# Recurrent chunks: the key and value tiles of four of eight heads turned by transposes

## The chip, the cores and the metric

One core of a Trainium2 chip runs the whole program in one launch. The metric is the device time of one execution in microseconds (us), the median of several runs. TensorE (PE) does matrix products and writes them to PSUM; its weight loads are shown apart as PEld. VectorE (DVE), ScalarE (ACT) and GpSimd (POOL) do the elementwise work; SyncE (SP) issues the DMAs. Each engine works through its own instructions in program order, and engines wait for one another by semaphores only.

## What is computed

Two layers of a first block (half an FFN, a mixer of pooling, convolution and neighbourhood attention, half an FFN) and then two layers of a second block (half an FFN, a mixer of three branches, attention over a memory, half an FFN), on 256 tokens of width 1024, in float32. The change touches one branch of the second block's mixer, the recurrence with 8 heads of 64 (`_rwkv_branch`):

```python
def step(state, inp):
    r_t, w_t, k_t, v_t, kk_t, a_t = inp
    sa = jnp.einsum('bhij,bhj->bhi', state, kk_t)
    state = (state * w_t[:, :, None, :]
             - sa[..., None] * (kk_t * a_t)[:, :, None, :]
             + v_t[..., None] * k_t[:, :, None, :])
    return state, jnp.einsum('bhij,bhj->bhi', state, r_t)
```

The kernel does not step through the 256 tokens. It takes them in 4 chunks of 64: within a chunk the products of keys with keys, the inverse of a triangular 64x64 matrix and the outputs are small matrix products, and a state of 64x64 per head goes from chunk to chunk.

## The kernel before, in words

Big products (FFN, projections) take each weight piece of 512 KB from DRAM into `raw`, ACT rounds it to a high part `w_hi` (L764), DVE or POOL computes the rest `w_lo` (L989), and PE forms three products per tile (L398 to L400, L414 to L416, L526 to L529).

The recurrence is `pe_rwkv` (L1742), `act_rwkv` and `dve_rwkv`; PE runs it once per layer of the second block, so twice, with 4 chunks each: 8 chunks. The 8 heads lie in pairs: head tile `t` (0 to 3) holds one head on partitions 0 to 63 and one on partitions 64 to 127. `HEADS` lists them as (t, first half), (t, second half), t by t, and every loop of a chunk goes in that order. An operand on the second half writes PSUM on partitions 64 to 127, so that all products of a chunk are 64 rows by 64 columns of the array, on one corner of it or on the opposite one.

A chunk goes through these stages on PE, in this order:

1. Turning (L1749 to L1753): for each head three 64x64 tiles (values `rz`, keys `rw_c[2]` and `rw_c[3]`) are multiplied with a 64x64 piece of the identity matrix in `const`, which leaves each tile's transpose in PSUM (banks 0 and 1). 24 products per chunk; the last raises `rw_turned`. ACT then copies them to `rw_tok` (L1852, L1854).
2. Grams (L1758 to L1763), products of keys with keys and queries, masked by DVE (L1911).
3. One piece of filling: `fill(1)` does a quarter of the gate projections that are to be done anyway, whole-array products at L398 to L400.
4. The chunk's right-hand side (L1780, L1781), which needs `rw_tok`, then five rounds of matrix powers and the inverse (L1789, L1791, L1799), each round with a quarter piece of filling between, while ACT and DVE copy the powers.
5. Outputs and new state (L1805 to L1827). After the last of them (`rw_y`, L1827) the turning of the next chunk follows in the program with one wait, for `rw_chunk_in`, which DVE raised long before.

Nothing in the order is planned at run time: the order on PE is the order of the program text.

Of the kernel before, what the change touches and what calls it, by code (L numbers as in the profile page):

```python
# [83 lines left out]
def const_layout():  # L84

    at, n = {}, 0
    for name, width in (("ident", P), ("na_mask", GRID), ("pool_cnt", 2 * S), ("causal", 2 * S), ("eps_ln", 1), ("eps_ln4", 1),
                        ("eps_rms", 1), ("eps_rms4", 1), ("eps_gn", 1), ("eps_0", 1), ("inv_freq", 1),
                        ("rope_sign", 1), ("halves", P), ("gla_full", 256), ("gla_half", P), ("strict", P),
                        ("lower", CHUNK), ("eye2", CHUNK), ("gather", 2), ("gather_g", 1),  # L90
                        ("spread", 512)):
        at[name] = n
        n += width
    return at, n


CONST, CONST_N = const_layout()
# [48 lines left out]
def build(nc, a, out, stop=None):  # L146
    ctx = ExitStack()
    with ctx:
        def sb(name, shape, dt=F32):
            return ctx.enter_context(nc.sbuf_tensor(name, shape, dt))  # L150
# [3 lines left out]
        def sem(name):  # L154

            if name not in sems:
                sems[name] = ctx.enter_context(nc.semaphore(name))
            return sems[name]
# [12 lines left out]
        ps = ctx.enter_context(nc.psum_tensor("ps", [P, 8, 512], F32))  # L171
# [5 lines left out]
        const = sb("const", [P, CONST_N])  # L177
# [44 lines left out]
        def cst(name, n, p=P):  # L222
            return const[0:p, CONST[name]:CONST[name] + n]

        ident = cst("ident", P)
# [1499 lines left out]
        W = CHUNK  # L1725
# [16 lines left out]
        def pe_rwkv(pe, fill):  # L1742
            pe.wait_ge(sem("rw_scaled"), 1)
            for n in range(CHUNKS):
# [4 lines left out]
                for t, o in HEADS:  # L1749
                    for b, src in enumerate((rz[o, 8 + t, 1 + n * W:1 + (n + 1) * W], rw_c[o, 2, t, :], rw_c[o, 3, t, :])):  # L1750
                        col = (b % 2) * 4 * W + t * W
                        mm = nc.tensor.matmul(ps[o, b // 2, col:col + W], src, const[o, CONST["ident"] + o.start:
                                              CONST["ident"] + o.stop], start=True, stop=True)  # L1753
                mm.then_inc(sem("rw_turned"), 1)
                if n:

# [1 line left out]
                for t, o in HEADS:  # L1758
                    for bank, keys in ((4, rw_bh), (6, rw_kh)):
                        nc.tensor.matmul(ps[o, bank, 2 * W * t:2 * W * (t + 1)].rearrange("p (a c) -> p a c", a=2),  # L1760
                                         keys[o, t, at], rw_pr[o, t, :, at], start=True, stop=True)
                    mm = nc.tensor.matmul(ps[o, 7, t * W:(t + 1) * W], rw_pr[o, t, 0, at], rw_bh[o, t, at], start=True,
                                          stop=True)  # L1763
# [4 lines left out]
                def power(i, t, o):  # L1768

                    return (rw_pow[o, 2 * (i % 2), t, :],  # L1770
                            rw_pow[o, 2 * (i % 2) + 1, t, :] if i else rw_g[o, 0, t, 0:W])
# [6 lines left out]
                for t, o in HEADS:  # L1778
                    x = ps[o, 7, t * W:(t + 1) * W]
                    nc.tensor.matmul(x, rw_c[o, 0, t, :], rw_st[o, t, :], start=True, stop=False)  # L1780
                    mm = nc.tensor.matmul(x, rw_g[o, 1, t, 0:W], rw_tok[o, 0, t, :], start=False, stop=True)  # L1781
                mm.then_inc(sem("rw_x"), 1)
                for i in range(1, POWERS + 1):
# [3 lines left out]
                    for t, o in HEADS:  # L1787
                        a, b = power(i - 1, t, o)
                        mm = nc.tensor.matmul(ps[o, 0, t * W:(t + 1) * W], b, a, start=True, stop=True)  # L1789
                        if i < POWERS:  # L1790
                            mm = nc.tensor.matmul(ps[o, 1, t * W:(t + 1) * W], a, b, start=True, stop=True)  # L1791
# [6 lines left out]
                    for t, o in HEADS:  # L1798
                        mm = nc.tensor.matmul(ps[o, 5, t * W:(t + 1) * W], power(i, t, o)[0], rw_t[o, (i - 1) % 2, t, :],  # L1799
                                              start=True, stop=True)  # L1800
# [13 lines left out]
                for t, o in HEADS:  # L1814
                    mm = nc.tensor.matmul(ps[o, 0, t * W:(t + 1) * W], rw_t[o, POWERS % 2, t, :], rw_x[o, t, :], start=True,
                                          stop=True)
# [3 lines left out]
                for t, o in HEADS:  # L1820
                    nc.tensor.matmul(ps[o, 5, t * W:(t + 1) * W], rw_tok[o, 1, t, :], rw_tok[o, 0, t, :], start=(t == 0),
                                     stop=False, skip_group_check=True)
                pe.wait_ge(sem("rw_u_taken"), n + 1)
                for t, o in HEADS:
                    y, state = ps[o, 4, t * W:(t + 1) * W], ps[o, 5, t * W:(t + 1) * W]
                    nc.tensor.matmul(y, rw_u[o, t, :], rw_g[o, 0, t, W:2 * W], start=False, stop=True, skip_group_check=True)
                    mm = nc.tensor.matmul(state, rw_tok[o, 2, t, :], rw_u[o, t, :], start=False, stop=True,  # L1827
                                          skip_group_check=True)
# [11 lines left out]
            for t in range(4):  # L1840
                o = ps[:, 6 + t // 2, (t % 2) * S:(t % 2 + 1) * S]
                nc.tensor.matmul(o, w_rgate[:, 0, t * P:(t + 1) * P], rz[:, 13, 1:], start=True, stop=False)
                mm = nc.tensor.matmul(o, w_rgate[32:64, 1, t * P:(t + 1) * P], rz[32:64, 14, 1:], start=False, stop=True)
# [141 lines left out]
        def _(pe):  # L1985
# [73 lines left out]
            for l in range(LAYERS):  # L2059
# [8 lines left out]
                pe_mla(pe, fill)  # L2068
                pe_gla(pe, fill)
                pe_rwkv(pe, fill)  # L2070

                pe.wait_ge(sem("att_out"), PAIRS)
# [748 lines left out]
```

## Time and profile before

| | us |
|---|---|
| median of 3 runs (lowest, highest) | 2659.61 (2659.55, 2663.37) |
| the profiled execution, by itself | 2660.73 |
| its span, first to last instruction | 2658.9 |
| what lies around the span in that execution | 1.8 |
| mean granted clock of TensorE | 0.997 |

A profile is one execution. A record of PE has a start, and an end that is modelled, so that the busy time of PE says that it had work in flight and not that the array was full; starts and the distances between them are the safer reading. A float32 product appears as two records (two passes over the array), with a weight load (PEld) each. "64\*64 64x64" is a record with 64 rows and 64 columns of weights, whose result is 64 partitions by 64 elements. The granted clock is 1.00 at 2.4 GHz and 0.50 at 1.2 GHz. "..." in a block of rows marks rows left out.

### The profile page before, as it was taken

How to read it: one execution, taken by the hardware profiler on the slowest of the kernel's cores; microseconds unless marked ns; L12 is line 12 of the kernel's file. 1: busy time of each engine (PE TensorE's matmuls, PEld its weight loads, DVE VectorE, ACT ScalarE, POOL GpSimd, SP SyncE). 2: the span in 40 equal slices, each digit the busy share in tenths (PEclk: the TensorE clock that was granted, in tenths of full speed). 3: DMA queues.
4: the chain of work that ended last, by engine and by line, in shares of the span. 5: the costliest groups of instructions: out<-in, count | busy, mean ns of one | idle time of the engine just before them, and what ended most of it. 6: DMA issues, size and time to landing. Idle time of an engine off the chain costs nothing.

```text
span 2658.9 us, 47077 instructions
## 1 busy us (share of the span) xinstructions
PE 2612.7 (98%) x18468; PEld 2302.3 (87%) x18468; DVE 1810.2 (68%) x2923; ACT 1386.2 (52%) x2186; POOL 218.4 (8%) x95
## 2 busy tenths in 40 slices
PE   9999999999999999999999999999999999999999
PEld 7889788888978888889999898888888999988887
DVE  6667766766777677767732856777775953475777
ACT  5456644544564454456524556446446642455544
POOL 0000000000000000015225000000003422300000
PEclk9999999999999999999999999999999999999999
DMA  8875466577546656663413655665674421564564
GB/s 254 235 195 170 134 189 190 177 225 200 173 134 190 190 151 205 190 190 113 123 49 119 198 168 156 191 190 176 189 213 128 133 84 51 176 201 138 176 189 134
DMA packets 613672, 444.52 MB, mean 167 GB/s; under 512 B 28224, under 2 KB 573536, under 8 KB 613024
## 3 DMA queue, kind: packets, MB, share of 16 engines
q1 hardware_dynamic: 613536, 442.62, 56.5%
q8 instruction: 96, 1.57, 0.2%
q14 instruction: 40, 0.33, 0.0%
HBM read 441.51 MB, written 1.05 MB: 166 GB/s over the span
## 4 chain that ended last, share of the span: by engine, by line
PE 88%; DVE 8%; ACT 1%; issue 1%; DMA 0%; POOL 0%; DVEq 0%; SPq 0%; ACTq 0%
PE ps L526 23%; PE ps L529 11%; PE ps L398 8%; PE ps L414 7%; PE ps L399 7%; PE ps L400 7%; PE ps L415 7%; PE ps L416 7%; DVE w_lo L989 2%; PE ps L1799 1%; PE ps L1789 1%; PE ps L711 1%; PE ps L1760 1%; PE ps L1791 1%; PE ps L749 1%
## 5 line engine op out<-in xcount | busy, mean ns | idle before, releaser
L989 DVE TENSOR_TENSOR w_lo<-raw,w_hi 128x1024 fp32r<-128x1024 f32 x700 | 855.9, 1224 | 396.8 <-ACT w_hi L764 395.4
L764 ACT ACTIVATE w_hi<-raw 128x1024 fp32r<-128x1024 f32 x796 | 840.1, 1056 | 455.2 <-PE ps L416 226.8
L526 PE MATMUL ps<-in_both,w_hi 128*128 128x512 f32 x2688 | 843.3, 395 | 1.3 <-DVE w_lo L989 1.3
L529 PEld LDWEIGHTS ps<-in_both,w_lo 128*128 128x128 f32 x2688 | 504.9, 188 | 117.7
L529 PE MATMUL ps<-in_both,w_lo 128*128 128x256 f32 x2688 | 528.1, 278 | 0.0
L398 PE MATMUL ps<-in_both,w_hi 128*128 128x256 f32 x1632 | 476.1, 292 | 20.2 <-DVE in_both L1060 7.4
L399 PE MATMUL ps<-in_both,w_hi 128*128 128x256 f32 x1632 | 462.8, 284 | 0.0
L400 PE MATMUL ps<-in_both,w_lo 128*128 128x256 f32 x1632 | 462.6, 283 | 0.0
L526 PEld LDWEIGHTS ps<-in_both,w_hi 128*128 128x128 f32 x2688 | 421.0, 189 | 14.8 <-DVE w_lo L989 2.5
L808 ACT ACTIVATE work<-ps 128x256 f32<-128x256 f32 x336 | 129.6, 386 | 524.5 <-PE ps L529 524.5
L989 POOL TENSOR_TENSOR w_lo<-raw,w_hi 128x1024 fp32r<-128x1024 f32 x90 | 217.9, 2429 | 2069.4 <-ACT w_hi L764 2069.4
L398 PEld LDWEIGHTS ps<-in_both,w_hi 128*128 128x128 f32 x1632 | 313.6, 192 | 30.3 <-issue 7.1
L399 PEld LDWEIGHTS ps<-in_both,w_hi 128*128 128x128 f32 x1632 | 313.7, 192 | 1.0 <-issue 0.5
L400 PEld LDWEIGHTS ps<-in_both,w_lo 128*128 128x128 f32 x1632 | 313.5, 192 | 0.0
L414 PE MATMUL ps<-w_hi,hid_hi 128*128 128x512 f32 x704 | 276.0, 392 | 2.2 <-DVE ps L1186 2.2
L415 PE MATMUL ps<-w_lo,hid_hi 128*128 128x512 f32 x704 | 274.6, 390 | 0.0
L416 PE MATMUL ps<-w_hi,hid_lo 128*128 128x512 f32 x704 | 274.0, 389 | 0.0
L1079 DVE TENSOR_TENSOR work<-ps,work 128x256 f32<-128x256 f32 x336 | 142.0, 423 | 96.4 <-ACT work L808 92.4
L416 PEld LDWEIGHTS ps<-w_hi,hid_lo 128*128 128x128 f32 x704 | 132.2, 188 | 28.6
L414 PEld LDWEIGHTS ps<-w_hi,hid_hi 128*128 128x128 f32 x704 | 132.0, 187 | 27.0 <-DVE ps L1186 3.5
L415 PEld LDWEIGHTS ps<-w_lo,hid_hi 128*128 128x128 f32 x704 | 132.2, 188 | 20.8
L1037 DVE TENSOR_TENSOR in_both<-arena,in_both 128x512 fp32r<-128x512 f32 x44 | 31.6, 744 | 89.3 <-ACT in_both L770 89.1
(362 smaller groups left out, 2837.7 us busy)
## 6 DMA issues: line engine op xcount, KB each, us to landing
raw<-in_w_ffn_in SPq DMA_DIRECT2D x176, 512.0 KB, 3.8
raw<-in_w_mix SPq DMA_DIRECT2D x108, 512.0 KB, 3.9
raw<-in_ffn_w_gate SPq DMA_DIRECT2D x88, 512.0 KB, 4.1
raw<-in_ffn_w_up SPq DMA_DIRECT2D x88, 512.0 KB, 3.8
raw<-in_ffn_w_down SPq DMA_DIRECT2D x88, 512.0 KB, 4.2
raw<-in_w_ffn_out SPq DMA_DIRECT2D x88, 512.0 KB, 4.2
raw<-in_w_in SPq DMA_DIRECT2D x40, 512.0 KB, 3.8
raw<-in_w_out SPq DMA_DIRECT2D x32, 512.0 KB, 3.6
```

The source lines that it names most:

```text
L398: nc.tensor.matmul(o, lh, rh, start=first, stop=False, **kw)
L399: nc.tensor.matmul(o, lh, rl, start=False, stop=False, **kw)
L400: return nc.tensor.matmul(o, ll, rh, start=False, stop=last, **kw)
L414: nc.tensor.matmul(o, left_hi[:, tok], right_hi, start=first, stop=False, **kw)
L415: nc.tensor.matmul(o, left_hi[:, tok], right_lo, start=False, stop=False, **kw)
L416: return nc.tensor.matmul(o, left_lo[:, tok], right_hi, start=False, stop=last, **kw)
L526: nc.tensor.matmul(bank.rearrange("p (a t) -> p a t", a=2), hi[:, k, :], in_both[:, k, :, :], start=(k == 0), stop=False, skip_group_check ...
L529: mm = nc.tensor.matmul(bank[:, 0:S], lo[:, k, :], in_hi[:, k, :], start=False, stop=(k == KD - 1), skip_group_check=True)
L764: nc.scalar.activation(w_hi[:, e % SPLIT, :], raw[:, e % RAW, :], ACT.Copy).then_inc(sem("split_high"), 1)
L808: nc.scalar.activation(part[:, j % 2, i, :], gate_up_bank(j, i)[:, S:2 * S], ACT.Copy)\
L989: eng.tensor_tensor(w_lo[:, e % SPLIT, :], raw[:, e % RAW, :], w_hi[:, e % SPLIT, :].bitcast(F32), ALU.subtract)\
L1079: nc.vector.tensor_tensor(o, gate_up_bank(j, i)[:, 0:S], part[:, j % 2, i, :], ALU.add).then_inc(sem("summed"), 1)
```

## The change

In the turning stage the heads on partitions 0 to 63 use TensorE's transpose instruction, with the same operands and the same place in PSUM; the heads on partitions 64 to 127 keep the product. The order of the 24 instructions stays, and so does the semaphore, which the last product (second half of t = 3) still raises.

```diff
                 for t, o in HEADS:
                     for b, src in enumerate((rz[o, 8 + t, 1 + n * W:1 + (n + 1) * W], rw_c[o, 2, t, :], rw_c[o, 3, t, :])):
                         col = (b % 2) * 4 * W + t * W
-                        mm = nc.tensor.matmul(ps[o, b // 2, col:col + W], src, const[o, CONST["ident"] + o.start:
-                                              CONST["ident"] + o.stop], start=True, stop=True)
+                        eye = const[o, CONST["ident"] + o.start:CONST["ident"] + o.stop]
+                        if o.start == 0:
+                            nc.tensor.transpose(ps[o, b // 2, col:col + W], src, eye)
+                        else:
+                            mm = nc.tensor.matmul(ps[o, b // 2, col:col + W], src, eye, start=True, stop=True)
                 mm.then_inc(sem("rw_turned"), 1)
```

Per chunk that makes 4 groups of 3 transposes and 4 groups of 3 products, in turn.

## Rows read from the trace of the kernel before

**Rows 1.** The page: busy time, share of the span, instructions; chain of work by engine.

```profile
span 2658.9 us, 47077 instructions
PE 2612.7 (98%) x18468; PEld 2302.3 (87%) x18468; DVE 1810.2 (68%) x2923; ACT 1386.2 (52%) x2186; POOL 218.4 (8%) x95
...
PE 88%; DVE 8%; ACT 1%; issue 1%; DMA 0%; POOL 0%; DVEq 0%; SPq 0%; ACTq 0%
```

**Rows 2.** Windows, four chunks of a layer: us, busy of PE, PEld, DVE, ACT, POOL, PEclk, DMA.

```profile
1316.50:1339.50 23.00, 23.00 (x500) 21.72 (x501) 8.77 (x19) 6.91 (x13) 8.01 (x4) 1.00 0.32 91
1339.50:1362.50 23.00, 23.00 (x510) 21.76 (x508) 8.39 (x20) 6.17 (x12) 4.73 (x2) 1.00 0.23 68
...
1385.50:1408.50 23.00, 23.00 (x510) 21.76 (x505) 8.19 (x17) 7.71 (x14) 7.47 (x3) 1.00 0.18 49
```

**Rows 3.** Waits in 1316.5 to 1408.5: who for whom, us in total, times, longest.

```profile
POOL w_lo L989 <- ACT w_hi L764: 67.5, 11, 13.0
ACT yT L1860 <- PE ps L1791: 22.0, 16, 2.1
...
ACT work L1852 <- PE ps L1752: 4.0, 4, 1.1
```

**Rows 4.** All records of line 1752 (turning), by operand: ns min/median/max, starts, form.

```profile
L1752 PE MATMUL ps<-const,arena x128: 218/218/268, 1316.5 to 2224.7; 64*64 64x64 f32 x128
L1752 PE MATMUL ps<-const,work x128: 218/218/218, 1316.7 to 2202.0; 64*64 64x64 f32 x128
L1752 PE MATMUL ps<-const,zT x128: 218/218/218, 1339.7 to 2225.0; 64*64 64x64 f32 x128
```

**Rows 5.** Timeline of PE at the second chunk's turning: start us, us, line, operands, records.

```profile
1339.45 0.33 PE L1827 MATMUL ps<-yT,work 64*64 64x64 f32 x4
1339.57 0.28 PE L1752 MATMUL ps<-const,arena 64*64 64x64 f32 x2
1339.68 0.22 PE L1752 MATMUL ps<-const,zT 64*64 64x64 f32 x1
1339.69 0.27 PE L1752 MATMUL ps<-const,arena 64*64 64x64 f32 x1
...
1339.92 0.22 PE L1752 MATMUL ps<-const,arena 64*64 64x64 f32 x1
...
1340.27 0.22 PE L1752 MATMUL ps<-const,arena 64*64 64x64 f32 x1
...
1340.97 0.27 PE L1760 MATMUL ps<-arena 64*64 64x128 f32 x1
1341.02 0.22 PE L1752 MATMUL ps<-const,zT 64*64 64x64 f32 x1
1341.08 0.27 PE L1760 MATMUL ps<-arena 64*64 64x128 f32 x1
1341.08 0.22 PE L1752 MATMUL ps<-const,zT 64*64 64x64 f32 x1
```

**Rows 6.** Timeline of PE, a turn by 16 transposes (L459), and what follows it.

```profile
1554.90 1.91 PE L459 MATMUL ps<-const,zT 128*128 128x128 f32 x16
1556.57 0.48 PE L398 MATMUL ps<-w_hi,in_both 128*128 128x512 f32 x1
```

**Rows 7.** Timeline of PE in four short stretches of line 1563 (products of two forms in turn).

```profile
2111.67 0.33 PE L1563 MATMUL ps<-arena 64*64 64x64 f32 x4
...
2111.93 0.33 PE L1563 MATMUL ps<-arena 64*128 64x64 f32 x2
...
2112.09 0.28 PE L1563 MATMUL ps<-arena 64*128 64x64 f32 x2
...
2112.30 0.27 PE L1563 MATMUL ps<-arena 64*64 64x64 f32 x2
```

**Rows 8.** Timeline of PE after the last chunk of the second layer, the first wait.

```profile
2256.91 0.28 PE L400 MATMUL ps<-in_both,w_lo 128*128 128x256 f32 x1
2258.58 0.39 PE L398 MATMUL ps<-in_both,w_hi 128*128 128x256 f32 x1 [1.39 <-POOL w_lo L989]
```

**Rows 9.** Windows as in rows 2: two turns by transposes, line 1563's stretch, what follows each.

```profile
978.95:983.77 4.82, 2.54 (x16) 1.65 (x16) 4.69 (x10) 2.94 (x7) 0.00 (x0) 0.94 0.01 3
983.77:986.68 2.91, 2.89 (x14) 2.89 (x14) 2.91 (x7) 2.91 (x6) 0.00 (x0) 0.51 0.56 175
986.68:989.59 2.91, 2.91 (x27) 2.91 (x26) 1.19 (x4) 2.17 (x6) 0.00 (x0) 1.00 0.36 97
200.44:204.53 4.09, 2.79 (x19) 1.93 (x18) 3.39 (x9) 3.76 (x9) 0.00 (x0) 1.00 0.14 40
204.53:207.40 2.87, 2.86 (x24) 2.87 (x25) 2.77 (x6) 2.87 (x6) 0.00 (x0) 1.00 0.43 130
2110.59:2114.01 3.42, 3.42 (x50) 2.88 (x49) 3.08 (x6) 3.36 (x7) 0.00 (x0) 1.00 0.02 5
2114.01:2117.40 3.39, 3.39 (x30) 3.39 (x29) 3.19 (x8) 1.25 (x3) 0.00 (x0) 1.00 0.94 273
...
2123.90:2130.10 6.20, 6.20 (x23) 5.42 (x24) 3.30 (x10) 6.16 (x8) 0.00 (x0) 0.50 0.59 168
```

## The prediction

> **What bounds the kernel now.** I read the page first: PE is busy 98% of the span, and 88% of the chain that ended last is PE [rows 1]. A mean over 2659 us says nothing about one stage, so the windows of the four recurrent chunks of a layer come next: each chunk is 23.0 us and PE has work in flight for all of them [rows 2]. The waits of that stretch name ACT, DVE and POOL as the ones that wait, mostly for PE; no line of that list has PE waiting [rows 3]. PE's order thus sets the length of a chunk, and each 0.1 us that PE's turning stage gets shorter or longer moves the end by as much. What ACT takes from the turning (L1852) waits for PE about 1 us per chunk, and PE needs its copies only after the grams and a piece of filling, so a later `rw_turned` makes no wait of its own: what comes after it on PE is delayed along with it.
>
> **How the turning runs now.** 384 records in 8 chunks are 48 per chunk for 24 products, two passes each [rows 4]. The timeline shows two streams side by side: after the start at 1339.57 the first half's tiles (each six passes of one head) begin anew at 1339.92 and 1340.27, so one half makes six passes in 0.35 us, 0.058 us per pass, and the other half makes its six in the same 0.35 us, a little behind [rows 5]. 48 passes therefore take only 24 passes' time: from 1339.57 to the last start at 1341.08, 1.51 us. There is no pause at either end: the state products before it (L1827) and the grams after it (L1760) overlap with it [rows 5], since all have the same 64\*64 form. In a layer's first chunk it is 0.05 us more, 1.56 us.
>
> **What the change removes.** 12 of the 24 products become transposes, and a transpose has one pass: 16 transposes of a turn are 16 records [rows 6]. From the first of them to what follows, (1556.57 - 1554.90) / 16 = 0.104 us go to a pass of 128 columns; I estimate half of it, 0.05 us, for 64 columns, near the pace of the product's pass, and use 0.06. So 12 passes of 48 go. If both halves still ran side by side, that would save next to nothing: the second half keeps its 24 passes of 0.058 us, 1.40 us, and they are the longer stream.
>
> **What it adds.** Each of the transposes in this trace is 128\*128, a use of the whole width of the array [rows 6]; no row shows one on 64 of 128 columns. The nearest form with 64 rows and the whole width is 64\*128, and this trace has one place where 64\*64 and 64\*128 products follow one another in turn, line 1563 [rows 7]. There a 64\*64 group starts at 2111.67; its last passes start 0.33 - 0.22 = 0.11 us later (0.22 is the length of one, rows 4), at 2111.78; the 64\*128 group starts only at 2111.93. So 0.15 us lie between the last start of one form and the first start of the other, where the same form follows at 0.058 us, and beside no other work. The first pass of the new form hides no weight load either: its second starts 0.11 us after it in the 64\*64 form, 0.16 us (2112.09 - 2111.93) in the 64\*128 form, and from there to the next 64\*64 start it is 0.21 us (to 2112.30). The change has three transposes and three products in turn, so 8 such switches in a chunk, one of them at its beginning.
>
> The Trainium skill, TensorEngine Tiling (Array Packing), section "Key Properties", says that changing the tiling mode, and not just the tile, drains the engine; its section "Restrictions and Gotchas" lists float32 transposes among what column tiling excludes. By the first, the 0.15 us of line 1563 are such a drain, and the trace agrees. By the second, a transpose cannot share the 64\*64 mode; no row of this trace shows that. It speaks against the change, for the same sum as below.
>
> **The sum.** T is a transpose, P a pass of a product, for one head tile t:
> T1 to T2 0.11 (weight load not hidden), T2 to T3 0.06, T3 to P1 0.15 (switch), P1 to P2 0.11, P2 to P6 4 x 0.058 = 0.23, P6 to the next T1 0.15 (switch): 0.81 us, where it was 0.35. First to last start in a chunk: 3 x 0.81 + 0.66 = 3.09 us (the last switch falls away, because the grams are 64\*64). In a layer's first chunk that is 3.09 - 1.56 = 1.53 us more; it follows filling of the 128\*128 form, so it enters by a switch before and after the change. In the other three it is 3.09 - 1.51 + 0.15 (the new switch after L1827) = 1.73 us more. One layer: 1.53 + 3 x 1.73 = 6.7 us; two layers: 13.4 us.
>
> The other end: if a transpose loads 128 columns of weights whatever it needs, its steps are those of the 64\*128 products, 0.16, 0.11 and 0.21 in place of 0.11, 0.06 and 0.15. Then a tile takes 0.97 us, first to last start is 3 x 0.97 + 0.82 = 3.73, a layer 2.17 + 3 x 2.37 = 9.3 and both 18.6 us. The lower end is the side-by-side case (first rival), -0.9 us. I take 13.4, as the weights that the change loads are 64 columns wide and a switch from 64-column passes has been seen to cost 0.15.
>
> The added time stays to the end. After the last chunk PE's first wait is 1.39 us for POOL's `w_lo` [rows 8], which waits for ACT's rounding, which waits for PE's own group means of that chunk: it moves along. If that wait vanished in both layers instead, 2.8 us would be given back; I leave it in. The filling's weights come no later, DMA being at 0.18 to 0.32 of its engines' time in these chunks [rows 2]. PE has no other work to put into the pauses, since its order is the program's.
>
> The profiled execution took 2660.73 us, 1.1 more than the median of 2659.61. 2660.7 + 13.4 = 2674.1 for a profile like it, and 2673.0 against the median, which is what I predict.
>
> **Rivals.**
> *Side by side as before.* Transposes of the first half run in the 64\*64 grouping beside the products of the second. For it: same operands, same corner of the array, and the trace has no 64-wide transpose to show otherwise. Against it: all transposes seen are of the whole width. Then the second half's 24 passes of 0.058 us set the stage as today, and the only gain is that they start earlier: their first record comes at 1339.69, 0.12 us behind the first half's, because six passes are queued ahead of it and not three. 8 x 0.12 = 0.9 us: 2658.7 us, not slower. It decides where a switch after a transpose costs under about 0.02 us.
> *The clock falls.* The stage would have 36 passes in 3.1 us in place of 48 in 1.5. In this trace a turn by transposes with a pause behind it was followed by a stretch of 2.9 us at a granted clock of 0.51 (1.2 GHz), in which PE started 14 records where the next 2.9 us at 1.00 have 27 [rows 9]: 13 x 0.108 = 1.4 us lost. Another fall lasted 6.2 us at 0.50 [rows 9], 3.1 us lost. In each of 8 chunks that is 11 to 25 us on top of 13.4: 2684 to 2698 us. Against it: a similar turn at 200.44 and line 1563's 3.42 us of switches were both followed by 1.00 [rows 9]; the latter is the nearest to what this change makes. The Trainium skill, TensorE: Matmul & The Clock Gate, section "Part 4: PE-mode transpose", says that transposes do not count as a busy PE for the clock; by that rule this case is likelier, and the two turns of rows 9 go one each way.
> *No pass saved.* The transpose of a 64-row tile takes two passes like the product: three more of 0.058 us per tile, 0.17 x 4 x 8 = 5.6 us on top, 2678.6 us. Against it are the 16 records for 16 transposes [rows 6].
>
> **Chances.** Forecast with its own range of 2671 to 2678.5: 0.78, with the third rival (0.04) at its upper end. Side by side: 0.10. Clock: 0.06. What remains, 0.02, is a stage that pays only half of the sum (+6.7 us, 2666.3). The range of 2666 to 2684 leaves out the first rival and most of the clock. A difference under 0.2% (5.3 us) cannot be told from no change here. Slower by over 0.2% are the forecast, the third rival, the clock and the half switch, 0.90; the same is the side-by-side case, 0.09; faster gets 0.01 for what I have not thought of.
>
> **What would show it.** In the profile after, the turning has 12 + 24 records per chunk; the transposes read 64\*64 or 64\*128, and no record of a product starts within 0.1 us of the last transpose; a chunk's period goes from 23.0 to 24.7 us; the granted clock stays at 1.00. I am wrong in the step of the switch if transposes and products start in pairs a few ns apart as they do now, in the step of the passes if there are 24 transposes' records in a chunk, and in the step of the clock if the chunks show 0.50.

## Result, and the profile after

The change makes the kernel slower: median 2674.99 us of 5 runs (2671.24 to 2676.47) against 2659.61 of 5 runs before; the ratio is 1.005, 95% interval 1.0039 to 1.0060. Run a second time, beside the kernel before (e0_again below), it was 2672.55 (5 runs) against 2660.74 (15 runs), ratio 1.0046 (1.0032 to 1.0059). The prediction was 2673.0. The profiled execution took 2671.24 us, its span is 2669.4. One of the ten executions of e1 below took 12318.96 us at a granted clock of 1.00, and the figures of e1 are those of the other nine.

The windows of the first two chunks and the fourth, which answer to [rows 2], with the same columns:

```profile
1316.05:1340.60 24.55, 24.55 (x491) 22.68 (x490) 8.73 (x19) 6.88 (x13) 7.98 (x4) 1.00 0.31 88
1340.60:1365.16 24.56, 24.56 (x493) 22.69 (x490) 8.38 (x20) 6.17 (x12) 4.73 (x2) 1.00 0.21 61
...
1389.71:1414.26 24.55, 24.55 (x493) 22.69 (x490) 8.18 (x17) 7.71 (x14) 7.60 (x3) 1.00 0.16 46
```

A chunk takes 24.55 us where it took 23.0. DVE and ACT are busy as long as before, PE has work in flight all the time as before, and the clock is 1.00. The timeline of PE at the second chunk's turning, which answers to [rows 5] (L1754 are the transposes, L1756 the products, L1830 the state products before and L1763 the grams behind):

```profile
1340.36 0.33 PE L1830 MATMUL ps<-yT,work 64*64 64x64 f32 x4
1340.62 0.24 PE L1754 MATMUL ps<-const,arena 64*64 64x64 f32 x1
1340.70 0.27 PE L1754 MATMUL ps<-const,zT 64*64 64x64 f32 x2
1340.90 0.32 PE L1756 MATMUL ps<-const,arena 64*64 64x64 f32 x2
1341.07 0.39 PE L1756 MATMUL ps<-const,zT 64*64 64x64 f32 x4
1341.39 0.24 PE L1754 MATMUL ps<-const,arena 64*64 64x64 f32 x1
1341.48 0.27 PE L1754 MATMUL ps<-const,zT 64*64 64x64 f32 x2
1341.68 0.33 PE L1756 MATMUL ps<-const,arena 64*64 64x64 f32 x2
1341.84 0.39 PE L1756 MATMUL ps<-const,zT 64*64 64x64 f32 x4
...
1343.45 0.28 PE L1756 MATMUL ps<-const,zT 64*64 64x64 f32 x2
1343.56 0.27 PE L1763 MATMUL ps<-arena 64*64 64x128 f32 x1
1343.57 0.22 PE L1756 MATMUL ps<-const,zT 64*64 64x64 f32 x1
```

What to see: three transposes, then six passes of products, then transposes again, and never two of them a few ns apart. The three transposes start at 1340.62, 1340.70 and (1340.70 + 0.27 - 0.22) 1340.75; the product behind them only at 1340.90, 0.15 us later. Its last pass starts at 1341.07 + 0.39 - 0.22 = 1341.24, and the next transposes at 1341.39, again 0.15 us later. A tile takes 1341.39 - 1340.62 = 0.77 us, where it took 0.35; first to last start is 1343.57 - 1340.62 = 2.95 us, where it was 1.51 [rows 5]. The form column says 64\*64 for both kinds, so it does not tell that they do not share the array; the starts do.

The records of the transposes, which answer to [rows 4] (times in ns, min/median/max):

```profile
L1754 PE MATMUL ps<-const,arena x32: 242/243/246, 1316.1 to 2234.9; 64*64 64x64 f32 x32
L1754 PE MATMUL ps<-const,work x32: 216/216/216, 1316.2 to 2210.5; 64*64 64x64 f32 x32
L1754 PE MATMUL ps<-const,zT x32: 216/216/216, 1340.7 to 2235.1; 64*64 64x64 f32 x32
```

96 records for 96 transposes: one pass each, as forecast. PE has 96 records fewer on the page (18372, before 18468 [rows 1]), and the kernel is slower all the same.

**Where the time came from.** A layer's first chunk has 2.95 - 1.56 = 1.39 us more, each of the other three 2.95 - 1.51 + 0.15 = 1.59 us, the last term being the new switch behind the state products (1340.62 against the last L1830 at 1340.47). That is 6.2 us a layer and 12.3 us in all. From the first turning of the second layer to the span's end it can be read off directly: 2658.9 - 2154.5 = 504.4 us before, 2669.4 - 2158.9 = 510.5 after, 6.1 us. The two profiled spans differ by 10.5 us only, because outside the recurrent chunks the clock was low for less time in the profile after. Windows of after, which answer to [rows 9]:

```profile
983.00:985.91 2.91, 2.27 (x19) 2.28 (x20) 2.91 (x9) 2.91 (x8) 0.00 (x0) 1.00 0.61 180
1286.60:1290.00 3.40, 3.40 (x13) 3.04 (x13) 3.26 (x9) 3.34 (x5) 0.00 (x0) 0.50 0.75 219
2119.46:2122.86 3.40, 3.40 (x18) 3.28 (x19) 3.06 (x8) 1.31 (x3) 0.00 (x0) 0.50 0.96 276
2122.90:2130.10 7.20, 7.20 (x54) 6.56 (x53) 6.70 (x16) 3.56 (x6) 0.00 (x0) 1.00 0.09 24
```

Before, the first of these places had 0.51 [rows 9], and the second had 1.00: these two falls are about as long and cancel. The last two stand where before had 0.50 for 6.2 us [rows 9] and 0.84 in the 2.0 us ahead of them; after has 0.50 for 3.4 us and then 1.00. By these rows before lost 3.1 + 0.3 us there and after 1.7, so 1.7 us came back, and 12.3 - 1.7 = 10.6 us is the difference of the spans. None of these stretches is in a recurrent chunk.

The same goes for executions without a profile, as far as their mean clocks tell: of the ten of the changed kernel in both comparisons, the one at 0.998 took 2670.95 us, those at 0.997 took 2671.24 to 2673.59, those at 0.996 took 2674.46 to 2676.47. The two medians of the changed kernel lie 15.4 and 11.8 us above those of before, on both sides of the 12.3; by the two ratios it is 13.3 and 12.2 us.

### The profile page after: what moved, and what is told of

Same layout as the page of the kernel before. It is cut to its first block, busy times and chain, and to the rows that moved or that the text cites. A ratio compares the mean times of both kernels' runs of the same rounds, so it can differ in the third digit from the quotient of the medians.

```text
span 2669.4 us, 46885 instructions
## 1 busy us (share of the span) xinstructions
PE 2623.2 (98%) x18372; PEld 2308.1 (86%) x18372; DVE 1810.5 (68%) x2923; ACT 1386.2 (52%) x2186; POOL 217.5 (8%) x95
## 3 DMA queue, kind: packets, MB, share of 16 engines
q8 instruction: 95, 1.56, 0.2%
HBM read 441.51 MB, written 1.05 MB: 166 GB/s over the span
## 4 chain that ended last, share of the span: by engine, by line
PE 89%; DVE 8%; ACT 1%; issue 1%; DMA 0%; POOL 0%; DVEq 0%; SPq 0%; ACTq 0%
PE ps L526 23%; PE ps L529 11%; PE ps L398 8%; PE ps L399 7%; PE ps L400 7%; PE ps L414 7%; PE ps L415 7%; PE ps L416 7%; DVE w_lo L989 1%; PE ps L1802 1%; PE ps L1792 1%; PE ps L711 1%; PE ps L1763 1%; PE ps L1794 1%; PE ps L749 1%
```

## Experiments

Theory S: a switch between the 64-wide form and the whole-width form costs 0.15 us, and across it the two halves cannot run side by side. Its rivals were that a transpose of a 64-row tile is dear by itself, and that only the loss of company counts (of the other half's passes, which ran beside).

**e1_grouped: 2 switches in a chunk in place of 8.** An edit of the changed kernel, like e2 and e5.

```diff
-                for t, o in HEADS:
+                for t, o in HEADS[0::2] + HEADS[1::2]:
```

> The changed kernel with the order of its turning stage altered: all 12 transposes of the first half, then all 12 products of the second, so 2 switches between the two kinds in a chunk and not 8. Theory S (a switch between the whole-width and the 64-wide form costs about 0.15 us, and the two halves cannot run side by side across it): 12 transposes 0.08 + 10 x 0.056 = 0.64, switch 0.15, 24 passes 0.11 + 22 x 0.058 = 1.39, so 2.18 us from first to last start where the changed kernel has 2.95 and the kernel before 1.51; 6 us slower than before in all. Rival T (a transpose of a 64-row tile is dear by itself, 1.55 us / 12 = 0.13 us each, wherever it stands): as the changed kernel, 2.95 us and 12 us slower than before.

Measured: 2.18 us from first to last start in every chunk, 23.78 us from chunk to chunk; median 2666.40 against 2660.80, 5.6 us more, ratio 1.0019 (1.0009 to 1.0029); the chunks alone make 6 us. PE's timeline, second chunk:

```profile
1342.93 0.24 PE L1754 MATMUL ps<-const,arena 64*64 64x64 f32 x1
1343.02 0.27 PE L1754 MATMUL ps<-const,zT 64*64 64x64 f32 x2
...
1343.52 0.27 PE L1754 MATMUL ps<-const,zT 64*64 64x64 f32 x2
1343.72 0.32 PE L1756 MATMUL ps<-const,arena 64*64 64x64 f32 x2
1343.89 0.39 PE L1756 MATMUL ps<-const,zT 64*64 64x64 f32 x4
```

Twelve transposes take 0.64 us (1342.93 to the last start at 1343.57); the one pause inside the stage is between 1343.57 and 1343.72. The same transposes in another order cost half: the transpose itself is not the dear part.

**e2_two_groups: 4 switches.**

```diff
-                for t, o in HEADS:
+                for t, o in [HEADS[i] for i in (0, 2, 1, 3, 4, 6, 5, 7)]:
```

> As the changed kernel, with the groups twice as long: 6 transposes, 6 products, 6 transposes, 6 products, so 4 switches in a chunk. Theory S: a pair of groups takes 0.08 + 4 x 0.056 + 0.15 + 0.11 + 10 x 0.058 + 0.15 = 1.29 us, so first to last start 1.29 + 1.14 = 2.43 us. Rival T: 2.95 us.

Measured: 2.43 us, 24.04 us from chunk to chunk. With 2, 4 and 8 switches the stage takes 2.18, 2.43 and 2.95 us: 0.13 us per added switch, as theory S has it: a pause of 0.15 in place of an ordinary spacing of 0.06, and 0.03 or 0.05 of a load that is no longer hidden. One execution took 2671.05 us; its chunks are 8.1 us longer in all than those of before.

The same figures part the two costs, as an estimate. Of the 8 switches 7 lie inside the stage, and 2.95 - 7 x 0.13 = 2.04 us is what it would take without them. That is about the sum of 12 transposes and 24 passes one after the other (12 x 0.056 + 24 x 0.058 = 2.06). So of the 1.44 us that the stage grew by, about 0.5 us is lost company and 0.9 us is switches; the rival that only company counts would have given 2.06 us and not 2.95.

**e3_products_grouped: the grouped order without transposes.** The edit of e1, on the kernel before.

> The kernel before (products only), in the grouped order: 12 products of the first half, then 12 of the second. No switch of form. If the halves run side by side only as far as PE looks ahead in its queue (2 to 3 passes, the lag seen between them), the stage takes nearly 48 passes of 0.058 us, 2.7 us from first to last start, 1.2 us more per chunk and 9 to 10 us more in all, so that half of the price of the changed kernel is lost company and not the switch. If the two halves have queues of their own of any depth, it stays at 1.5 us.

Measured: 2.56 us (2.61 in a layer's first chunk), 24.01 us from chunk to chunk; 2669.76 us in one execution. The halves hardly run side by side. PE's timeline where they meet:

```profile
1342.45 0.28 PE L1753 MATMUL ps<-const,arena 64*64 64x64 f32 x2
1342.57 0.22 PE L1753 MATMUL ps<-const,zT 64*64 64x64 f32 x1
1342.57 0.27 PE L1753 MATMUL ps<-const,arena 64*64 64x64 f32 x1
1342.62 0.22 PE L1753 MATMUL ps<-const,zT 64*64 64x64 f32 x1
1342.68 0.22 PE L1753 MATMUL ps<-const,arena 64*64 64x64 f32 x1
```

The second half's first record starts at 1342.57, when the first half has three passes left: the second half is reached only that late, and 48 passes take 2.56 us where interleaved heads take 1.51. In this order products are slower than e1's transposes (2.56 against 2.18). So a transpose does save passes; in the tuned order there is nothing to save, because those passes are covered.

**e4_first_half_out: only the second half is turned.** An edit of the kernel before, like e6.

```diff
-                for t, o in HEADS:
+                for t, o in HEADS[1::2]:
```

> The kernel before with the 12 products of the first half left out (those tiles are not turned, so the first four heads' results are not the reference's). The first half's products are covered by the second half's: 24 passes of 0.058 us, 1.4 us from first to last start instead of 1.51, about 1 us less in all 8 chunks; that is the most that any cheaper way of turning the first half alone could give. If PE's passes of the two halves were instead one queue at 0.029 us each, the stage would halve to 0.7 us and 6 us would be saved in all.

Measured: 1.39 us in a layer's first chunk and 1.34 in the others, 22.85 us from chunk to chunk (before 22.98). Half of the work taken out is worth 0.13 us a chunk, 1.0 us in all: the ceiling of any cheaper way to turn the first half alone. The one execution took 2660.71 us where those of before took 2657.87 to 2665.52, which cannot show 1 us; the starts can.

**e5_wide_products: whole-width products in place of the transposes.**

```diff
+                flat = rw_c.rearrange("p b t c -> p (b t c)")
                 for t, o in HEADS:
...
                         if o.start == 0:
-                            nc.tensor.transpose(ps[o, b // 2, col:col + W], src, eye)
+                            lo = 19072 + (8 + t) * (S + 1) + 1 + n * W
+                            lo2 = min(4 * W * (b + 1) + t * W, 14 * W)
+                            wide = arena[o, lo:lo + 2 * W] if b == 0 else flat[o, lo2:lo2 + 2 * W]
+                            nc.tensor.matmul(ps[:, b // 2, col:col + W], wide, eye, start=True, stop=True)
```

> The kernel before, in its order, with no transposes; the 12 products of the first half take 128 columns of weights (the tile and what lies behind it) and so have the form 64*128; the products of the second half come after them and write over the columns that are too many. One of the 12 tiles is taken 64 columns too early, so one head's result is not the reference's. Theory S (the form matters, not the transpose): a pause of 0.2 us before each group of 64*64 products and 0.15 us before each 64*128 group, never a pair of records a few ns apart; a tile takes 0.16 + 4 x 0.111 + 0.21 + 0.11 + 4 x 0.058 + 0.15 = 1.30 us, first to last start 5.05 us. Rival T2 (the pauses belong to the transpose instruction): no pauses, 6 x 0.111 + 6 x 0.058 = 1.01 us per tile, or less where the halves run side by side; 4.0 us or less from first to last start.

Measured, in the chunk whose turning ran most nearly at full clock: 5.16 us; the other seven, with more of it at half clock, took 5.29 to 6.62. Its timeline:

```profile
2238.20 0.43 PE L1758 MATMUL ps<-const,arena 64*128 64x64 f32 x2
2238.47 0.61 PE L1758 MATMUL ps<-const,work 64*128 64x64 f32 x4
2239.01 0.33 PE L1760 MATMUL ps<-const,arena 64*64 64x64 f32 x2
2239.17 0.39 PE L1760 MATMUL ps<-const,work 64*64 64x64 f32 x4
2239.50 0.43 PE L1758 MATMUL ps<-const,arena 64*128 64x64 f32 x2
```

A tile takes 1.30 us. The pauses stand where the form changes, with no transpose in the program: from the last wide start (2238.47 + 0.61 - 0.27 = 2238.81) to 2239.01 it is 0.20 us, from the last narrow one (2239.34) to 2239.50 it is 0.16. It is the change of form that costs. The execution took 2710.46 us, about 50 us more than before, where turnings of 5.05 us explain 29 (1.56 or 1.51 before, and 0.15 for the new switch). The rest had been a rival of the prediction, the clock. Windows of this kernel, three in the first chunk, then two around the turning shown:

```profile
1316.80:1320.80 4.00, 4.00 (x39) 3.53 (x37) 1.23 (x1) 1.29 (x2) 3.29 (x2) 1.00 0.75 223
...
1322.20:1325.00 2.80, 2.80 (x36) 2.80 (x35) 0.00 (x0) 0.87 (x2) 0.00 (x0) 0.52 0.57 166
1325.00:1328.00 3.00, 3.00 (x37) 2.93 (x34) 1.92 (x4) 0.00 (x0) 0.00 (x0) 1.00 0.00 0
2238.20:2243.36 5.16, 5.16 (x53) 4.69 (x51) 0.85 (x2) 0.38 (x1) 0.00 (x0) 0.97 0.01 3
2243.36:2246.50 3.14, 3.14 (x38) 3.14 (x37) 0.00 (x0) 0.87 (x2) 0.00 (x0) 0.50 0.00 0
```

In all 8 chunks the clock fell to 1.2 GHz in the turning or at its end, and what followed, the grams in the chunk of 2238, ran at half the rate. The eight stretches at 0.50 are 43.7 us long together, and half of that, 22 us, is lost: with the 29 it is about the 50.

**e6_pairs_in_filling: an attempt to beat both.** Both heads of a tile are turned by one transpose, 12 in a chunk, ahead of the filling.

```diff
                 mm.then_inc(sem("rw_grams"), 1)
+                pe.wait_ge(sem("rw_chunk_in"), 2 * n + 1)
+                pe.wait_ge(sem("rw_state"), n + 1)
+                for t in range(4):
+                    for b, src in enumerate((rz[:, 8 + t, 1 + n * W:1 + (n + 1) * W], rw_c[:, 2, t, :], rw_c[:, 3, t, :])):
+                        mm = nc.tensor.transpose(ps[0:W, (0, 1, 5)[b], 2 * W * t:2 * W * (t + 1)], src, ident)
+                mm.then_inc(sem("rw_turned"), 1)
                 fill(1)
```

The turning at the chunk's head is gone, and ACT copies each half of `rw_tok` for itself.

> A version meant to beat both kernels: 12 transposes per chunk turn both heads of a tile at once (128 partitions by 64 columns, whole width), placed after the grams, just ahead of the filling, which is of the 128*128 form anyway; ACT moves each head's part to its own half by 4 copies where there were 2. Theory S: no switch is added, the stage of 1.40 us goes, 12 passes of 0.056 us (0.64 us) come, and the filling's first pass is 0.1 us less late: a chunk takes 22.98 - 1.40 + 0.64 + 0.05 - 0.10 = 22.2 us, 6.5 us less in all, about 2653 to 2654 us. If the 128-row transposes of 64 columns are a form apart from the filling's, one more switch of 0.15 to 0.2 us: 22.4 us per chunk, 4.7 us less. Rival: ACT's copies (4 of 0.4 to 0.6 us, 2.0 us together) come after the filling of 2.9 us has ended, and PE waits for them; then a wait of PE for ACT shows ahead of the right-hand side.

A miss: 23.55 us from chunk to chunk, median 2663.78 against 2660.74, ratio 1.0012 (1.0003 to 1.0021). Its timeline, the wide transposes with the filling, an ordinary 128\*64 product with the filling, and the head of a chunk:

```profile
1344.95 0.30 PE L1762 MATMUL ps<-const,arena 128*64 128x128 f32 x1
1345.08 0.38 PE L1762 MATMUL ps<-const,zT 128*64 128x128 f32 x2
1345.30 0.27 PE L1762 MATMUL ps<-const,arena 128*64 128x128 f32 x1
...
1346.18 0.27 PE L1762 MATMUL ps<-const,zT 128*64 128x128 f32 x1
1346.20 0.36 PE L398 MATMUL ps<-in_both,w_hi 128*128 128x256 f32 x1
...
1262.28 0.28 PE L749 MATMUL ps<-work,sq 128*64 128x128 f32 x2
1262.49 0.39 PE L398 MATMUL ps<-in_both,w_hi 128*128 128x256 f32 x1
...
1342.32 0.32 PE L1753 MATMUL ps<-arena 64*64 64x128 f32 x1 [0.47 <-ACT work L1864]
```

One part held: a transpose of 64 columns is followed by the whole-width filling at once (1346.18 to 1346.20), where a product of the same form leaves 0.2 us (1262.28 to 1262.49). So a float32 transpose of 128 rows and 64 columns goes with the whole-width form, whatever its form says, and being a transpose is not what costs: in [rows 6] the filling follows 16 transposes as closely (the last starts at 1554.90 + 1.91 - 0.27 = 1556.54, the filling at 1556.57). For the 64-row tiles of the change this is not shown. In the changed kernel a layer's first chunk goes from filling to transposes:

```profile
1315.74 0.28 PE L399 MATMUL ps<-in_both,w_hi 128*128 128x256 f32 x1
1315.86 0.28 PE L400 MATMUL ps<-in_both,w_lo 128*128 128x256 f32 x1
1316.07 0.24 PE L1754 MATMUL ps<-const,arena 64*64 64x64 f32 x1
```

That is 0.21 us where two passes of filling lie 0.12 apart, and it was 0.21 with a product in the place of the transpose. So a 64-row transpose follows neither the filling nor the 64-wide products without a pause.

Two terms of e6 failed. I had priced a pass at 0.056 us as in the change, but each of these transposes has a result 128 columns wide and takes (1346.18 - 1344.95) / 11 = 0.11 us, so the 12 passes are 1.3 us, nearly as long as the stage that they replace. And the grams, now at the head of the chunk, wait 0.47 us for ACT's copy of the outputs (L1864), which the turning used to cover. The rival, a wait of PE for ACT ahead of the right-hand side, did not show. No run here beats the kernel before by more than can be measured.

**e0_again: the changed kernel once more.**

> The changed kernel once more, unaltered. The stage itself is set by PE's order and should be the same to 0.01 us in every chunk: 2.95 us from first to last start, 24.55 us from chunk to chunk, 12.3 us more than before in all. If the rest of the difference between the medians (15.4 us) belongs to the change, it comes again here, above 14 us; if it is a matter of where the clock falls in a single execution, the difference over many runs lies nearer to 12 us, and the spans differ between executions by several us with the same chunks.

Measured: 2.95 us and 24.55 us in every chunk again, median 11.8 us above before. The excess of the first comparison did not come back.

## Why the prediction was right, step by step

- *PE's order sets the length of a chunk*: right. All of 1.39 or 1.59 us per chunk arrives at the end, and PE's wait for POOL behind the chunks is 1.4 us as in [rows 8].
- *One pass per transpose*: right, 96 records. The rival of two passes is out. The pace was read a little low: from [rows 6] I took the start of what follows as the end, but it comes 0.03 us after the last start. From start to start a pass of 128 columns takes (1556.54 - 1554.90) / 15 = 0.109 us and not 0.104; half of it is 0.055, and 0.056 was measured.
- *A switch between the forms costs 0.15 us*: right, and read from products of another line [rows 7]. The changed kernel has 0.15 us in both directions; e1 and e2 show that the price goes with the number of switches, e5 that it comes without transposes. By the Trainium skill, TensorEngine Tiling (Array Packing), section "Restrictions and Gotchas", float32 transposes are excluded by column tiling; the trace of e6 agrees, with 0.02 us where a 64-column product leaves 0.2.
- *T1 to T2 0.11 us*: too dear. It is 0.08, and T2 to T3 0.056 where I put 0.06. That is the whole miss of the stage: 0.77 us per tile and not 0.81, 2.95 us and not 3.09, 12.3 us in all and not 13.4.
- *The end at 18.6 us*, for a load of 128 columns: out; the step after a transpose's first pass is even shorter than the 0.11 of a 64-column product, and the switch from a transpose to a product takes 0.15 and not 0.21.
- *Side by side*: out, as no product starts within 0.14 us of a transpose. e4 shows that it would have been worth about 1 us at most, near the 0.9 that I had put on it (8 x 0.12 is 0.96).
- *The clock*: out for this change, with 1.00 in every recurrent chunk. It was no idle rival: e5's turnings of 5.2 us and more lost the clock, the change's 2.95 us did not.
- *The median*: 2673.0 is 13.4 above before, and the stage gave 12.3. That the two medians, 15.4 and 11.8 above before, lie on both sides of 13.4 is chance: they moved 3.6 us with the same chunks.

## What to carry to other kernels

Before replacing an instruction by a cheaper one, look at the starts of its neighbours: if two streams run side by side, passes taken from one of them are worth next to nothing (e4: 1 us for half of the work). A change of form in the middle of a stage is a term of its own, here a pause of 0.15 us where 0.06 is usual, and it is priced from any place in the trace where the two forms already alternate; if both kinds are needed, group them. The form column of a record does not tell which forms can share the array; the distances between starts do.

## What the runs showed of the hardware that was not expected

PE reaches the other half's work only about three passes ahead: in e3 the second half starts when the first has three passes left, which makes interleaving heads worth 1.05 us in 2.56. And a stage that keeps PE busy by its records can be followed by half the clock: in e5, with PE in flight all the time, the granted clock fell to 0.50 in or at the end of all 8 turnings, which would take 5.05 us at full clock. With as many switches and fewer, shorter passes in 2.95 us, it stayed at 1.00 in all 16 chunks profiled (the two profiles of the changed kernel). No run varied the length, the passes and the pauses apart, so which of them lost the clock in e5 stays open.
